# Putting the high and low activations side by side in five projections, and gathering the narrow products of the up projections

## The reference

```python
for l in range(2):
    x = x + 0.5 * ((silu(h @ w1) * (h @ w3)) @ w2)          # h = rmsnorm(x), width 1024 -> 2816
    h = rmsnorm(x, g_mix[l])
    q_sb, k_sb, v_sb, q_r, k_r, v_r, g_r, u_p, gate = split(h @ w_in[l])
    y_sb   = stick_breaking_attention(q_sb, k_sb, v_sb)     # z = q k^T; log_beta; exp(log_beta + after)
    y_ret  = retention(rotary(q_r), rotary(k_r), v_r, g_r)
    y_pool = pool_mixer(u_p)
    x = x + (gates * branches) @ w_out[l]
    x = x + 0.5 * ((silu(h2 @ w1) * (h2 @ w3)) @ w2)
```

## Time and profile before

| | |
|---|---|
| median of 3 runs | 1572.39 us |
| the profiled execution | 1571.86 us, of which the span of the trace 1570.1 us |
| TensorE matmul | busy 1553.3 us, 99% of the span, 8958 matmuls |
| VectorE | busy 1114.1 us, 71% |
| ScalarE | busy 865.8 us, 55% |
| GpSimd | busy 102.0 us, 6% |
| memory read | 302 MB, 193 GB/s over the span |

### The profile page before, as it was taken

The page is one execution under the profiler, slowest core; times in us unless marked ns, Lnnn a source line. Parts: engine busy times, 40 slices in busy tenths (PEclk is TensorE's granted clock), DMA queues, the critical chain, the costliest instruction groups (busy, mean ns, idle before and its releaser), DMA issues.

```text
span 1570.1 us, 22403 instructions
## 1 busy us (share of the span) xinstructions
PE 1553.3 (99%) x8958; PEld 1355.4 (86%) x8958; DVE 1114.1 (71%) x1422; ACT 865.8 (55%) x1006; POOL 102.0 (6%) x100
## 2 busy tenths in 40 slices
PE   9999999999999999999999999999999999999998
PEld 7988898888888888898889888888888988888887
DVE  7889767888778666666667666676666667676665
ACT  8878574665575444564446444554445644464443
POOL 1135300000000000010100000000000101000000
PEclk9999999999999999999999999999999999999999
DMA  8889966355556555454544555455554555546552
GB/s 302 256 228 279 281 183 228 126 203 188 211 161 241 200 180 188 161 187 172 207 180 157 211 188 196 153 215 190 186 188 155 183 186 191 186 173 214 188 189 79
DMA packets 44063, 305.75 MB, mean 195 GB/s; under 512 B 5056, under 2 KB 5440, under 8 KB 7744
## 3 DMA queue, kind: packets, MB, share of 16 engines
q1 hardware_dynamic: 39696, 279.55, 48.8%
q0 software_dynamic: 3264, 22.02, 6.8%
q10 hardware_dynamic: 1008, 2.82, 0.5%
HBM read 302.27 MB, written 1.05 MB: 193 GB/s over the span
## 4 chain that ended last, share of the span: by engine, by line
PE 88%; DVE 5%; DMA 3%; ACT 2%; issue 1%; SPq 0%; POOL 0%; POOLq 0%; ACTq 0%; DVEq 0%
PE pairs L892 22%; PE pairs L899 11%; PE pairs L671 8%; PE pairs L672 8%; PE pairs L673 8%; PE big L671 7%; PE big L673 7%; PE big L672 7%; PE pairs L913 3%; DMA wlo<-weights 2%; DVE wlo L586 1%; DVE ar L1880 1%; PE pairs L921 1%; DVE ar L1888 1%; PE big L722 1%
## 5 line engine op out<-in xcount | busy, mean ns | idle before, releaser
L586 DVE TENSOR_TENSOR wlo<-raw,whi 128x2048 fp32r<-128x2048 f32 x239 | 546.4, 2297 | 182.2 <-ACT whi L572 179.8
L572 ACT ACTIVATE whi<-raw 128x2048 fp32r<-128x2048 f32 x259 | 492.8, 1910 | 130.0 <-PE big L673 74.1
L892 PE MATMUL pairs<-h_both,whi 128*128 128x512 f32 x1600 | 407.7, 392 | 0.4 <-DVE wlo L586 0.3
L892 PEld LDWEIGHTS pairs<-h_both,whi 128*128 128x128 f32 x1600 | 290.4, 189 | 53.0 <-DVE wlo L586 1.3
L899 PEld LDWEIGHTS pairs<-h_both,wlo 128*128 128x128 f32 x1600 | 218.3, 190 | 15.6
L1415 ACT ACTIVATE ar<-pairs 128x512 f32<-128x512 f32 x135 | 80.1, 596 | 263.6 <-PE pairs L892 223.5
L899 PE MATMUL pairs<-h_both,wlo 128*128 128x256 f32 x1600 | 223.1, 282 | 0.0
L671 PE MATMUL big<-whi,b_hi 128*128 128x512 f32 x452 | 177.6, 393 | 0.5 <-DVE wlo L586 0.4
L673 PE MATMUL big<-whi,b_lo 128*128 128x512 f32 x452 | 176.2, 390 | 0.0
L672 PE MATMUL big<-wlo,b_hi 128*128 128x512 f32 x452 | 175.9, 389 | 0.0
L1880 DVE TENSOR_TENSOR ar<-pairs,ar 128x512 f32<-128x512 f32 (+1 forms) x120 | 88.0, 734 | 90.4 <-ACT ar L1415 88.6
(11 more groups left out here) (265 smaller groups left out, 2088.6 us busy)
## 6 DMA issues: line engine op xcount, KB each, us to landing
raw<-weights SPq DMA_DIRECT2D x262, 1024.0 KB, 4.8
wlo<-weights POOLq DMA_DIRECT2D x20, 1024.0 KB, 14.2
ar<-consts ACTq DMA_DIRECT2D x1, 1536.0 KB, 9.4
ar<-mem SPq DMA_DIRECT2D x2, 512.0 KB, 5.5
raw<-weights SPq DMA_DIRECT2D x4, 256.0 KB, 6.1
x_rows<-x SPq DMA_DIRECT2D x1, 1024.0 KB, 10.6
ar<-ar POOLq DMA_DIRECT2D x8, 128.0 KB, 3.5
ar<-ssm_bc SPq DMA_DIRECT2D x1, 512.0 KB, 13.5
```

Source lines behind the costliest of these rows:

```text
L572: act.activation(whi[:, slot(u), :], raw[:, u % RING, :], ACT.Copy).then_inc(S("hi_done"), 1)
L586: dve.tensor_tensor(wlo[:, slot(u), :], raw[:, u % RING, :], whi[:, slot(u), :].bitcast(F32), ALU.subtract)\
L892: return pe.matmul(out, w(k, l, (half * KD + kk) * P, P)[0], h_both[:, kk, :, :].rearrange("p a t -> p (a t)"), start=kk == 0, stop=kk == ...
```

## The change

The five units get a routine of their own, `wide_unit`. It multiplies `whi` with the 512 columns of `h_both`, as `up` does, and `wlo` with the 256 columns of `h_hi`. A 128-wide column block now fills a whole bank (256 columns of high and 256 of low activations), so a unit takes two banks. ScalarE copies the second half of each bank, VectorE then adds the first half (`joined`), and that frees the bank. In `wide_unit` and in `up` the 16 narrow matmuls stand in one run, with 9 wide ones before and 7 after.

```diff
+WIDE = (2, 3, 4, 5, 7)
-UNITS2 = [["rvu0"], ["rv0"], ["sbq"], ["sbk"], ["rq"], ["rk"], ["sbv"], ["up"], ["rgu0", "rgu1"],
+UNITS2 = [["rvu0"], ["rv0"], ["sbq0", "sbq1"], ["sbk0", "sbk1"], ["rq0", "rq1"], ["rk0", "rk1"], ["sbv"], ["up0", "up1"], ["rgu0", "rgu1"],
...
-                place_read(pool, "rq", l)
-                place_read(pool, "rk", l)
+                place_read(pool, "rq1", l)
+                place_read(pool, "rk1", l)
...
+            def wide_unit(k, l, names):
+                def high(m, kk):
+                    return pe.matmul(bank(names[m], l)[:, :], w(k, l, (m * KD + kk) * P, P)[0],
+                                     h_both[:, kk, :, :].rearrange("p a t -> p (a t)"), start=kk == 0,
+                                     stop=m == 1 and kk == KD - 1)
+                unit_in(k, l)
+                place_free(pe, names[0], l)
+                for kk in range(KD):
+                    high(0, kk)
+                place_free(pe, names[1], l)
+                high(1, 0)
+                for m in range(2):
+                    for kk in range(KD):
+                        last = pe.matmul(bank(names[m], l)[:, 0:TOK], w(k, l, (m * KD + kk) * P, P)[1], h_hi[:, kk, :],
+                                         start=False, stop=m == 0 and kk == KD - 1)
+                    if m == 0:
+                        fin(last)
+                for kk in range(1, KD):
+                    last = high(1, kk)
+                fin(last)
...
-                        for kk in range(KD - 1):
-                            both(kk)
-                        for kk in range(KD):
-                            pe.matmul(out[:, 0:TOK], w(k, l, (half * KD + kk) * P, P)[1], h_hi[:, kk, :],
-                                      start=False, stop=False)
-                        last = both(KD - 1)
+                    for kk in range(KD):
+                        both(0, kk, False)
+                    both(1, 0, False)
+                    for half in range(2):
+                        for kk in range(KD):
+                            low(half, kk, half == 0 and kk == KD - 1)
+                    for kk in range(1, KD):
+                        last = both(1, kk, kk == KD - 1)
...
-                        evac(name, {3: sbk, 4: rq, 5: rk, 6: sbv}[u], l)
+                    if u in WIDE:
+                        for m, job in enumerate(UNITS2[u]):
+                            job_done(act, job, l)
+                            copy(wide_out(u)[:, m * TOK:(m + 1) * TOK], bank(job, l)[:, TOK:], wide_scale(u))\
+                                .then_inc(S("wide_low"), 1)
...
+                def joined(u):
+                    for m, name in enumerate(UNITS2[u]):
+                        dve.wait_ge(S("wide_low"), 2 * (len(WIDE) * l + WIDE.index(u)) + m + 1)
+                        half = wide_out(u)[:, m * TOK:(m + 1) * TOK]
+                        stt(half, bank(name, l)[:, 0:TOK], wide_scale(u), half, ALU.mult, ALU.add)\
+                            .then_inc(read_sem(name, l), 1)
...
+                    if u in WIDE:
+                        joined(u)
                     if u < U_MIX2 - 1:
                         split_dve(dve, k, l)
                     if u == 6:
                         rotated()
```

More of the change, by code:

```diff
@@ L478, in build_program, with wide_out, wide_scale @@
         sum2, sum4, sum8, sum16 = (area(GT + 2048 + 512 * i, 512).rearrange("p (c t) -> p c t", c=2) for i in range(4))
+        def wide_out(u):
+            return {2: sbq, 3: sbk, 4: rq, 5: rk, 7: up}[u]
+        def wide_scale(u):
+            return 64.0 ** -0.5 if u == 2 else 1.0
         y_sq, y_n = area(W + 4608, 1024), area(R, 1024)
@@ L888, in up, with both, low @@
                     up_bank_free(par, i)
-                    for half in range(2):
[L890 to L894, removed]
-                        for kk in range(KD - 1):
-                            both(kk)
+                    def both(half, kk, stop):
+                        return pe.matmul(pairs[:, 2 * par + half, :], w(k, l, (half * KD + kk) * P, P)[0],
+                                         h_both[:, kk, :, :].rearrange("p a t -> p (a t)"),
+                                         start=kk == 0, stop=stop)
+                    def low(half, kk, stop):
+                        pe.matmul(pairs[:, 2 * par + half, 0:TOK], w(k, l, (half * KD + kk) * P, P)[1],
+                                  h_hi[:, kk, :], start=False, stop=stop)
+                    for kk in range(KD):
+                        both(0, kk, False)
+                    both(1, 0, False)
+                    for half in range(2):
                         for kk in range(KD):
-                            pe.matmul(out[:, 0:TOK], w(k, l, (half * KD + kk) * P, P)[1], h_hi[:, kk, :],
-                                      start=False, stop=False)
-                        last = both(KD - 1)
+                            low(half, kk, half == 0 and kk == KD - 1)
+                    for kk in range(1, KD):
+                        last = both(1, kk, kk == KD - 1)
                     fin(last)
@@ L1301, in sb_scores @@
                 def sb_scores():
-                    place_read(pe, "sbq", l)
-                    place_read(pe, "sbk", l)
+                    place_read(pe, "sbq1", l)
+                    place_read(pe, "sbk1", l)
                     place_free(pe, "z", l)
@@ L1388, in _ @@
                         w_out(k, l, l * 3 + 5)
+                    elif u in WIDE:
+                        wide_unit(k, l, names)
                     elif 1 < u < 26:
@@ L1818, in _ @@
                         evac("rv0", rv[:, 0, :], l)
-                    if u == 2:
-                        evac(name, sbq, l, scale=64.0 ** -0.5)
-                    if u in (3, 4, 5, 6):
-                        evac(name, {3: sbk, 4: rq, 5: rk, 6: sbv}[u], l)
+                    if u in WIDE:
[3 more added lines that the diff above has]
+                                .then_inc(S("wide_low"), 1)
+                    if u == 6:
+                        evac(name, sbv, l)
                     if u == 4:
@@ L1830, in _ @@
                     if u == 7:
-                        evac("up", up, l)
                         act.wait_ge(S("lf_ready"), l + 1)
@@ L2468, in rotated @@
                     tt(rqk, rqk, swapped, ALU.add).then_inc(S("rqk_rot"), 1)
+                def joined(u):
[4 more added lines that the diff above has]
+                            .then_inc(read_sem(name, l), 1)
                 def pooled():
-                    place_read(dve, "up", l)
+                    place_read(dve, "up1", l)
                     sums, src = (sum2, sum4, sum8, sum16), up2
```

## The result

The changed kernel takes 1584.48 us (median of 6 runs, 1584.09 to 1586.23) where the kernel before, run beside it, takes 1572.61 (6 runs, 1571.46 to 1573.25): 1.0079 times as long, 95% interval 1.0069 to 1.0089. Slower, as forecast, and 1.0 us above the predicted 1583.5. The profiled execution was the slowest of the six: 1586.23 us, with a span of 1584.4, 14.3 above the 1570.1 of before.

What follows compares the result with a forecast made beforehand. TensorE, busy 99% of the span, was taken to bound the kernel. From the profiled 1571.86 us, -1.7 + 9.8 + 3.0 gave 1583.0, or 1583.5 for the metric; likeliest case 1581.5 to 1585, 8 in 10 within 1574 to 1587.

Steps and rivals of the forecast that it cites:

- Term 3: Ahead of step 8, TensorE waits for VectorE's addition behind `rotated`, itself slowed by GpSimd's mask: +4.9 us per layer, +9.8.
- step 3: In the mixers, sbq0 is read out of this step's second bank 0.1 us late at worst; left out.
- Term 4: After the gap ahead of step 8, TensorE returns at the lower clock: 1.5 us per layer, +3.0.
- Term 1: `up` units of five feed-forwards each lose one of two wide-narrow pairs, 0.017 us each: -1.7 us.
- Term 2: Products of the five wide units take 5.57 us instead of 5.76 each: -0.95 us per layer.
- rival C: At step 8 no new wait decides and only the products count: 1568.8 us; chance 0.07.
- Rival A: Ahead of step 8 the clock doesn't fall, or only in one layer: 1580.5 (or 1582) us; chance 0.18.
- Rival B: Before step 8, an early swap lets `rotated` precede GpSimd's mask; gap 2.9 us, no clock fall: 1574.5 us; chance 0.12.
- Rival D: Around step 8 the clock stays low twice as long, or the swap lands later still: 1586 to 1588 us; chance 0.11.

Runs made afterwards that it cites:

- e3: Changed kernel with `rotated` moved behind step 7's additions, split and low parts on VectorE: 1569.0 us.
- e5: Changed kernel with step 7 narrow as before, its one result copied by ScalarE, steps 2 to 5 still wide: 1569.32 us.
- e6: Changed kernel with GpSimd's mask made to wait until `rotated` is done: 2.5 us above the expected 1573.2.
- e9: Changed kernel with 12 calls of an unread filler matmul ahead of step 8: median differs by 3.4 us from the changed kernel's.
- e1: Kernel before with only the `up` units rewritten, narrow matmuls in one run of 16: 1.2 us below before, ratio 0.9992.
- e7: Kernel before with each `up` unit's narrow matmuls in four runs of 4 instead of two of 8: 0.5 us more.
- e8: e3 with ScalarE copying the low half of sbq0 ahead of its split of step 2: 1568.58 us.
- e10: The edit of e3 to the changed kernel, run again beside e8: 1568.76 us.
- e2: Changed kernel with the `up` units in their old order, only the five wide units kept: ratio 1.0091.
- e4: Changed kernel with 25 calls of an unread filler matmul ahead of step 8, which it delayed by 4.4 us; no total time given.

## Why the prediction was right, step by step

- **Term 3, the wait: right in place, cause and size.** A 5.89 us interval from start to start ahead of step 8 in both layers (predicted: a gap of 5.9), released by the addition in the `ar` tile; step 8 starts 5.1 and 4.9 us later than before, counted from the head of the mixer (predicted +4.9; step 3's 0.3 and 0.2 are in it). e3 and e5 take it away by two different edits. The step back to its cause is right too: `rotated`'s first operation ends 1.1 us after the mask, and e6 shows that the mask is the reason. The 3.67 us of the earlier trace rows that I took for the mask alone are another GpSimd operation of the same shape; e6 has the mask itself with 3.49.
- **Term 4, the clock: the mechanism right, the size wrong.** I took 1.5 us per layer from the seven slow matmuls at the kernel's start; it is 2.9 and 2.1, by e9 2.8 and 2.1. The clock fell 5.2 us after the last matmul of step 7 began (3.5 in layer 1), still ahead of step 8, and stayed at 0.50 until 707.95. In layer 0 step 8's first interval is 0.565 us where e9 has 0.306, and 13 follow of 0.427 instead of 0.227, 2.9 us in all. The half rate lasted 6.1 and 4.45 us from step 8's start, not the "some 3 us" that I expected. The seven matmuls of the earlier trace rows were too short a sample. My bounds, 0 to 3 a layer, just hold it.
- **Term 1, the `up` units: right.** -1.7 predicted, -1.9 measured over five feed-forwards (in e1 too, whose whole span is 1.6 shorter). The explanation behind it, a fixed 17 ns for each pair of changes, holds for the runs of this kernel and not in general (e7).
- **Term 2, the products: right.** 5.567 us for an undisturbed wide unit, predicted 5.57. In e8, which has none of the waits, a mixer takes 66.30 and 66.31 us for 67.22: 0.9 less, predicted 0.95. e5's and e3's times say that this is what the wide units are worth, as rival C had it for a kernel without the wait: C's 1568.8 is e3's 1569.0 and e10's 1568.8.
- **Step 3, "0.1 us late at worst": too low.** 0.28 and 0.19 us in the changed kernel, 0.5 us of span in all; 0.03 to 0.7 in the other executions with this wait, none in e8.
- **Rival A, the clock doesn't fall:** refuted in both layers. Had it been so, e9 and the changed kernel would be alike.
- **Rival B, `rotated` overtakes the mask:** the landing, on which I had let it depend, did come early enough: at 692.72 and 1251.98, 1.8 and 0.6 us ahead of the split's end. It did not help, since the mask is released by VectorE's work on z and was there 2 us before `rotated`. B was wrong in this: with the mask already running, an early landing gives nothing. What decides is which of the two starts first. Where e6 forced the order, the gap was 2.6 us, close to B's 2.9. But B's "too short for the clock" is wrong: in layer 1 it fell.
- **Rival D, "the clock stays low for twice as long":** this half of D is what happened, since the clock cost 5.1 us in all and not 3.0. The profiled execution (1586.23) even lies in D's range, the median (1584.48) in that of my forecast.
- **What the profiled execution adds:** 1.1 us ahead of anything that the change touches. At 122.47 TensorE waits for a weight tile, 3.68 us from start to start where before it was 1.48 us, and the clock falls there also:

```profile
124.27:131.09 6.82, 4.94 (x23) 4.94 (x24) 6.65 (x11) 4.83 (x6) 5.39 (x4) 0.50 1.01 280
```

  The DMA engines are fully busy in it. The profiles of before, e1, e5, e6 and e8 have no such fall, that of e3 has one as long (6.8 us), those of e2, e4, e7, e9 and e10 one of 3.4 us. Both groups hold kernels with the wide units and kernels without (e7 has none), so the fall does not need the change. It varies between executions; what tips it is open, and so is how much of the 1.1 it makes: without a fall e5 and e8 are 0.8 and 0.7 us above before at the same place.

So 1571.86 - 1.9 + 10.0 + 5.1 + 1.1 = 1586.2, which is the profiled execution (the 10.0 is the later start of step 8 in both layers, with the products and step 3 in it). Against that execution the forecast's 1583.0 was 3.2 too low, 2.1 of it term 4 and 1.1 the mixers of the first block. That the metric came within 1.0 of the forecast is in part luck: the median lies 1.75 below the profiled execution of the changed kernel, where for the kernel before it lies 0.75 above.

## What to carry to other kernels

When a result gets a second reader on another engine, look at what stands ahead of that reader in its engine's order, above all anything that waits for a transfer or for GpSimd, and who reuses the bank; one call moved turned +0.8% into -0.2%. Price a gap on TensorE at its length plus the half-rate stretch behind it, here 2.1 to 2.9 us on 5.9, in the profiled executions. A TensorE at 98% says nothing on such a gap: read it from start to start.

## What the hardware showed that I had not expected

- The granted clock can fall behind a gap of 2.6 us (e6, layer 1, 1.6 us lost) and stay up behind an equal one (layer 0).
- It stayed at 0.50 for 6.8 us behind 5.9 us of waiting, in both layers, while matmuls followed one another without a pause for the last 4.5 to 6.1 us of it.
- The filler matmul, on fp32 and not on split operands, shows as two matmuls of 0.216 us each per call (24 for e9's 12 calls, in 5.34 us).
- Changing between 256 and 512 columns shows no single long interval. The five wide ones after a change are 1 to 9 ns slow, and the first two narrow ones are 1 to 7 ns fast.
